# Turning the attention probabilities on VectorE in 32 by 32 blocks, value products on 32 by 64 tiles, and normalising on ScalarE

## The chip, the cores and the metric

One core of a Trainium2 chip runs the whole program. The time is the device time of one execution in microseconds. Its engines are PE (TensorE, matrix products), DVE (VectorE), ACT (ScalarE), POOL (GpSimd) and SP (SyncE, which here only starts transfers). ACT can start transfers too.

## The reference

A sequence of 512 rows of width 2048 goes through two layers of a block, and then through a recurrent mixer. The attention of a layer is what the change touches:

```python
for i in range(DEPTH):                      # DEPTH = 2
    hn = _rmsnorm(h, norm_g[i])
    u = hn @ w_in[i]
    a_val, a_glu, a_z, q, k, v, b_z = jnp.split(u, offs, axis=-1)
    ya = _conformer_conv(a_val, a_glu, conv_w[i], conv_b[i], cln_g[i], cln_b[i])
    ya = ya * jax.nn.silu(a_z)
    # 16 query heads of 64, 4 key and value heads; blocks of 128 queries see 3 blocks of keys,
    # key and query at most 128 apart
    yb = _window_attention(q, k, v, bias_band, sink[i]) * jax.nn.silu(b_z)
    h = h + jnp.concatenate([ya, yb], axis=-1) @ w_out[i]
    e = _rmsnorm(p[i] @ w_pe[i], pe_g[i])
    h = h + e * jax.nn.sigmoid(h @ w_pg[i])

# in _window_attention, for one block of queries
s = jnp.einsum('bqkgd,bskd->bkgqs', qb, kb) * scale + bias_band      # masked with NEG
m = jnp.maximum(jnp.max(s, axis=-1), sink_f)
e = jnp.exp(s - m[..., None])
denom = jnp.sum(e, axis=-1) + jnp.exp(sink_f - m)
pr = e / denom[..., None]
out = jnp.einsum('bkgqs,bskd->bqkgd', pr, vb)
```

Behind the two layers stands `h + norm(rglru(norm(h)))` (projection, short convolution, gates, a scan over the rows, projection) and one more gate.

## The kernel before

**Main products.** Everything has its channels on the 128 partitions and the 512 rows in the columns. An f32 product is made of three: weights are split into a high part `WH` and a low part `WL`, activations into `XH` and `XL`, and `three` (L1533 to L1535) or `pair_unit` (L1557 to L1563) adds high by high, low by high and high by low over 128 by 128 weight tiles and 512 columns. Weights arrive in units of 512 KB in a ring of four: SP loads `raw`, ACT writes `WH` (`prep`, L527), POOL writes `WL` (L498), PE uses the unit up and counts `w_used`. Each engine has its own list of instructions, which it works off in the order of the code; semaphores tie the lists together.

**Attention in the z stage.** While PE makes the 16 tiles of z (the gates of both halves, `silu` on them), attention goes between the main products, eight pairs of heads `t` in each layer. The stage is cut into 25 steps `n` of 10, 10 and 11 weight tiles (`Z_CUTS`). After the step with n % 3 = 0, PE makes `values(n // 3 - 1)` and then `scores(n // 3)`; after the step with n % 3 = 2 it makes `turn(n // 3)`. DVE, ACT and POOL have the same loop over n; `UNITS_AT` says which units of weights end in which step.

- `scores(t)` (PE, L1721): per block of 128 queries b and head hh, 64 by 64 tiles, 192 to 320 keys wide. The order of the blocks is `BLOCKS` (1, 2, 0, 3). Results stand in the PSUM tiles sc (b = 1), att and stat (b = 2), tr (b = 0 and 3).
- DVE adds the bias to them, finds the maximum and writes them to SBUF (L1130); ACT makes the exponentials and their sums (`exps`, L663, and the sink's, L666).
- `finish(t)` (DVE): adds the sums (L1136), takes the reciprocal (L1138) and multiplies the eight tiles of probabilities by it (L1144, L1149); each counts `probs_ready`.
- `turn(t)` (PE, L1731): 20 transposes of 128x128 against the identity, into the PSUM banks of the scores.
- `probs_out(t)` (ACT, L680 and L685): copies them to SBUF, to the turned tiles (`TX`, inside H and an own tile); `pt_ready`.
- `values(t)` (PE, L1742): 20 calls of 64 keys by 64 channels of a head. Tiles of the first 64 keys of each block add up in bank `TR[0]`, those of the last 64 in `TR[1]` (`VALUE_STEPS` gives key block and columns of each).
- `att_out` (DVE, L1153) and `far_out` (ACT, L673) copy the two sums to SBUF, and before the gate DVE adds the two (L1162). The scores of block 0 of the next pair wait for both copies (`att_ready`, `att_far`), as they use those banks.

A matmul of f32 operands (scores and values) stands twice in the records for each call. The values `v` stand turned in H (tiles `VT`, `turn_values`, L1706, copied by ACT, L653).

**Behind the z stage** the output stage adds H from memory (`h_dma` on SP, four loads of 1 MB; `add_out`, L1201) to the products of the second group of weights. The last stage, B, has its own weights; ahead of it ACT takes roots for the norm (`root`, Sqrt).

Column sums for the norms are made from squares by adding tiles on DVE; the last addition of each sum goes to the SBUF tile `acc`, from which `split_low` makes the operand SPLIT of the statistics product (`stat`, L1599).

## Time and profile before

| | before |
|---|---|
| time, median of 3 runs | 2586.24 us (2586.16 to 2586.34) |
| profiled execution | 2586.3 us |
| its span | 2584.5 us |
| PE busy | 2576.5 us, 100% |
| DVE busy | 1350.7 us, 52% |
| ACT busy | 971.2 us, 38% |
| POOL busy | 1430.0 us, 55% |
| granted clock of PE | 1.00 |

The span runs from the first to the last instruction of the profiled execution; 1.8 us lie around it. Ends of matmuls are modelled, so two matmuls overlap in the records: of main products read the starts. A row "x6" in a timeline joins six neighbours of one kind; its length is that of all six.

### The profile page before, as it was taken

The numbers are of one execution on the slowest core, as the hardware profiler recorded it, in microseconds if no ns is written. First come the engines' busy times: TensorE is split into PE (matmuls) and PEld (weight loads), VectorE is DVE, ScalarE is ACT, GpSimd is POOL, SyncE is SP. The second block draws the span as 40 slices with busy tenths as digits, with TensorE's granted clock in tenths as the row PEclk, the third lists the DMA queues.
The fourth block names the chain that finished last, engine by engine and source line by source line (L and its number), as shares of the span: only waits on it lengthen the run. The fifth ranks groups of instructions, "written<-read, shape, count | busy, mean of one in ns | idle before, by whom it ended". The sixth has DMA issues, their size and how long they took to land.

```text
span 2584.5 us, 35219 instructions
## 1 busy us (share of the span) xinstructions
PE 2576.5 (100%) x12368; PEld 2116.8 (82%) x12368; DVE 1350.7 (52%) x2086; ACT 971.2 (38%) x1516; POOL 1430.0 (55%) x1812
## 2 busy tenths in 40 slices
PE   9999999999999999999999999999999999999999
PEld 7888888788888888888887888888888888888887
DVE  7877766540063277777665400633753664522722
ACT  5222355442162242223544321733422656423521
POOL 5555545455565555555444555555666777655664
PEclk9999999999999999999999999999999999999999
DMA  7322222242234332222232422333333222322232
GB/s 249 106 98 97 94 88 94 86 154 94 95 100 136 114 123 95 94 96 98 85 97 91 151 95 97 98 130 114 106 105 123 98 98 97 140 98 97 90 98 105
DMA packets 78100, 279.34 MB, mean 108 GB/s; under 512 B 8304, under 2 KB 15216, under 8 KB 74928
## 3 DMA queue, kind: packets, MB, share of 16 engines
q1 hardware_dynamic: 77856, 277.89, 32.1%
q8 instruction: 63, 1.03, 0.2%
q14 instruction: 37, 0.30, 0.0%
q10 hardware_dynamic: 144, 0.11, 0.0%
HBM read 265.36 MB, written 15.76 MB: 109 GB/s over the span
## 4 chain that ended last, share of the span: by engine, by line
issue 36%; POOL 34%; PE 28%; POOLq 0%; DMA 0%; ACT 0%; SPq 0%; DVE 0%; DVEq 0%
POOL WL L498 34%; PE acc L1533 7%; PE acc L1534 7%; PE acc L1535 7%; PE sc L1533 1%; PE sc L1534 1%; PE sc L1535 1%; PE sc L1559 1%; PE sc L1557 1%; PE sc L1563 1%; DMA raw<-in_w 0%; PE tr L1533 0%; PE tr L1534 0%; PE tr L1535 0%; POOL WL L503 0%
## 5 line engine op out<-in xcount | busy, mean ns | idle before, releaser
L498 POOL TENSOR_TENSOR WL<-raw,WH 128x256 fp32r<-128x256 f32 x1792 | 1414.2, 822 | 1121.3 <-ACT WH L527 1121.2
L527 ACT ACTIVATE WH<-raw 128x1024 fp32r<-128x1024 f32 x450 | 472.1, 1058 | 1191.3 <-PE acc L1535 681.6
L1533 PE MATMUL acc<-XH,WH 128*128 128x512 f32 x2128 | 831.6, 391 | 0.0
L1535 PE MATMUL acc<-XH,WL 128*128 128x512 f32 x2128 | 828.2, 389 | 0.0
L1534 PE MATMUL acc<-XL,WH 128*128 128x512 f32 x2128 | 828.1, 389 | 0.0
L1533 PEld LDWEIGHTS acc<-XH,WH 128*128 128x128 f32 x2128 | 399.4, 188 | 86.5 <-issue 4.5
L1535 PEld LDWEIGHTS acc<-XH,WL 128*128 128x128 f32 x2128 | 399.4, 188 | 83.7
L1534 PEld LDWEIGHTS acc<-XL,WH 128*128 128x128 f32 x2128 | 399.5, 188 | 81.8
L1533 PE MATMUL sc<-XH,WH 128*128 128x512 f32 x640 | 249.0, 389 | 0.8 <-POOL WL L498 0.8
L1535 PE MATMUL sc<-XH,WL 128*128 128x512 f32 x640 | 249.0, 389 | 0.0
L1534 PE MATMUL sc<-XL,WH 128*128 128x512 f32 x640 | 249.0, 389 | 0.0
L943 DVE SCALAR_TENSOR_TENSOR Y<-tr,lv,Y 128x503 f32 (+13 forms) x240 | 175.6, 732 | 2.3 <-DVE T L1038 2.2
L943 DVE SCALAR_TENSOR_TENSOR T<-acc,rs 128x512 f32<-128x512 f32 (+1 forms) x78 | 53.1, 682 | 235.8 <-PE acc L1535 235.8
L943 DVE SCALAR_TENSOR_TENSOR T<-tr,lv,T 128x498 f32<-128x498 f32 (+6 forms) x224 | 163.8, 731 | 0.0
L1533 PEld LDWEIGHTS sc<-XH,WH 128*128 128x128 f32 x640 | 120.1, 188 | 26.2 <-issue 1.2
L1535 PEld LDWEIGHTS sc<-XH,WL 128*128 128x128 f32 x640 | 120.1, 188 | 25.0
L1534 PEld LDWEIGHTS sc<-XL,WH 128*128 128x128 f32 x640 | 120.1, 188 | 24.8
L1557 PE MATMUL sc<-XH,WH 128*128 128x512 f32 x320 | 98.7, 390 | 0.0
L1559 PE MATMUL sc<-XH,WL 128*128 128x512 f32 x320 | 98.5, 389 | 0.0
L1559 PE MATMUL acc<-XH,WL 128*128 128x512 f32 x320 | 98.5, 389 | 0.0
L1563 PE MATMUL sc<-XL,WH 128*128 128x512 f32 x320 | 98.5, 389 | 0.0
L1563 PE MATMUL acc<-XL,WH 128*128 128x512 f32 x320 | 98.5, 389 | 0.0
(294 smaller groups left out, 2739.9 us busy)
## 6 DMA issues: line engine op xcount, KB each, us to landing
raw<-in_w SPq DMA_DIRECT2D x450, 512.0 KB, 3.3
h_spill<-H SPq DMA_DIRECT2D x8, 1024.0 KB, 6.0
H<-h_spill SPq DMA_DIRECT2D x8, 1024.0 KB, 7.4
a<-bias_band SPq DMA_DIRECT2D x16, 384.0 KB, 3.2
H<-in_x SPq DMA_DIRECT2D x5, 1024.0 KB, 10.7
bias_band<-bias_line SPq DMA_DIRECT2D x1, 3072.0 KB, 16.1
out<-H SPq DMA_DIRECT2D x3, 1024.0 KB, 8.0
H<-in_x SPq DMA_DIRECT2D x5, 512.0 KB, 8.7
```

The lines of the kernel that those rows point to most:

```text
L498: part = pool.tensor_tensor(WL[:, c], raw[:, c], WH[:, c].bitcast(F), ALU.subtract)
L527: act.activation(WH[:, c], raw[:, c], ACT.Copy).then_inc(wh_ready, 1)
L943: return dve.scalar_tensor_tensor(out_, in0, scalar, in1, op0, op1)
L1533: pe.matmul(bank, WH[:, c], xh, start=first, stop=False)
L1534: pe.matmul(bank, WH[:, c], xl, start=False, stop=False)
L1535: return pe.matmul(bank, WL[:, c], xh, start=False, stop=last)
L1557: pe.matmul(two[b][:, :], WH[:, cols[b]], tl(XH, kt), start=first, stop=False)
L1559: pe.matmul(two[b][:, :], WL[:, cols[b]], tl(XH, kt), start=False, stop=False)
L1563: low = pe.matmul(two[b][:, :], WH[:, cols[b]], tl(XL, kt), start=False, stop=final)
```

## The change

- `turn` and `probs_out` are gone. `block_turns(t)` on DVE, in the step n % 3 = 2, turns each 32 by 32 block of the probabilities in its place (`dve.transpose`, 16 instructions a pair, 12 of 128 and 4 of 256 columns): the rows of a turned tile are then the keys of a group i of 32 within each 128, and the columns are ordered by key block, group of 32 queries and query.
- `values(t)` takes one row group of 32 partitions for each i. Row group i holds, for each group k of 32 queries, its probabilities for keys in the blocks near by, and reads `value_part(g, k)`, the values laid out for it. It makes 16 steps x 4 row groups x 2 heads = 128 calls on tiles of 32 rows by 64 columns, 32 to 96 columns wide, 992 columns in all for each tile (1088 before), into four banks `VALUE_BANKS`: att (`VB`), stat (`N`), and the two of tr.
- The layout of the values for this is made once a layer by transfers on ACT's queue (`value_copies`): one of 512 KB to `v_spill` in memory, then 12 reads, 2 MB in all, in pieces of 512 bytes; `v_out`, `vr_in`.
- The reciprocal stays on DVE (`recip_ready`), the eight multiplications go to ACT (`norms`, at the beginning of the step n % 3 = 2).
- `att_out` copies banks 0 and 1 on DVE, `far_out` banks 2 and 3 on ACT, each 128x128, straight to the tile of H. The addition L1162 is gone. The scores of block 2 wait for DVE's two, those of block 0 for ACT's two. The gated result of attention stays in H (`silu`, `xhigh`, `xlow`).
- SP: loads 2 and 3 of H in the output stage are issued behind four more weight units and a wait for `xl_ready`.
- Sums of squares stay in PSUM (`VB`) and are no longer copied to `acc`; at the start the squares are taken in another order (`X_LEAD` 11, `first_square`, `half_high`); in stage B `prep(B0, 1)` and `prep(B0, 2)` stand ahead of `root`, and `prep(B0, 3)` ahead of the second Sqrt.

The diff, without the sums and with the renamed tiles left out:

```diff
+def value_steps(i):
+
+    def seen(k):
+        near = [b for b in range(NB) if abs(4 * b + i - k) <= 4]
+        return k, near[0], near[-1] + 1
+
+    return [seen((i + s) % GROUPS_OF) for s in (12, 0, *range(1, 12), 13, 14, 15)]
...
+        def turned(hh, k, b0, b1):
+
+            o, lo, n = queries_of(k // 4)
+            c = o * BLK + (k % 4 * n + b0 - lo) * QB
+            return TX[hh][:, c:c + (b1 - b0) * QB]
+
+        def turned_to(hh, b, kb, blocks):
+
+            o, lo, n = queries_of(kb)
+            nxt = queries_of(kb + 1) if blocks == 2 else (o, lo, n)
+            step = (nxt[0] - o) * BLK + (lo - nxt[1]) * QB
+            return bass.AP(TXT[hh], o * BLK + (b - lo) * QB, [[TXW[hh], P], [step, blocks], [n * QB, 4], [1, QB]])
...
+        def value_part(g, k):
+
+            if g == 0:
+                return Y, (CT * S + k * P)
+            return (Y, 12 * S + k * P) if k < 12 else (H, VT * S + (k - 12) * P)
...
+        VALUE_BANKS = (VB, N, TR[0], TR[1])
...
                 for c in range(4):
+                    if c == 2:
+                        pair_units(u0, OUT0 + RING, OUT0 + 8)
+                        sp.wait_ge(xl_ready, ly * (3 * NT) + 2 * NT)
                     if ly:
                         sp.wait_ge(h_out[c], ly * 16)
                     h_dma(c, False, ly == 0)
-                pair_units(u0, OUT0 + RING, OUT0 + 8)
...
                 def far_out(t):
 
                     act.wait_ge(pv_done, ly * CT + (t + 1))
-                    act.activation(tl(Y, CT + t), TR[1][:, :], ACT.Copy).then_inc(att_far, 1)
-
-                def probs_out(t):
-                    base = ly * (2 * PAIRS) + 2 * NB * t
-                    for hh in range(2):
-                        for b in (0, 3):
-                            act.wait_ge(tr_done, base + 2 * hh + 2)
-                            act.activation(turned_of(b, hh), sbank(b, hh).rearrange("p (k q) -> p k q", q=BLK),
-                                           ACT.Copy).then_inc(pt_ready, 1)
-                    for b in (1, 2):
+                    for i in (2, 3):
+                        act.activation(att_part(t, i), VALUE_BANKS[i][:, 0:BLK].rearrange("p (b q) -> p b q", q=QB),
+                                       ACT.Copy).then_inc(att_far, 1)
+
+                def norms(t):
+                    act.wait_ge(recip_ready, ly * CT + (t + 1))
+                    st = sm[:, 24 * (t % 2):24 * (t % 2) + 24]
+                    for c, b in enumerate(BLOCKS):
                         for hh in range(2):
-                            act.wait_ge(tr_done, base + (2 * b + hh + 3))
-                            act.activation(turned_of(b, hh), sbank(b, hh).rearrange("p (k q) -> p k q", q=BLK),
-                                           ACT.Copy).then_inc(pt_ready, 1)
+                            k = 8 + 4 * hh + c
+                            act.activation(pbuf(b, hh), pbuf(b, hh), ACT.Copy, scale=st[:, k:k + 1]).then_inc(probs_ready, 1)
+
+                def value_copies():
+
+                    act.wait_ge(v_out, ly * 16 + 16)
+                    for g in range(2):
+                        for i in range(4):
+                            for kb0, kb1 in ((0, 4),) if g == 0 else ((0, 3), (3, 4)):
+                                buf, c = value_part(g, 4 * kb0)
+                                act.dma_start(buf[i * QB:(i + 1) * QB, c:c + (kb1 - kb0) * S].rearrange("p (k c) -> p k c", c=P),
+                                              bass.AP(v_dram, kb0 * BLK * 2 * P + g * P,
+                                                      [[2 * P, QB], [QB * 2 * P, 4 * (kb1 - kb0)], [1, P]])).then_inc(vr_in[g], 16)
 
                 values_out(0)
                 values_out(1)
+                act.wait_ge(v_ready, ly * 2 + 2)
+                act.dma_start(bass.AP(v_dram, 0, [[2 * P, P], [BLK * 2 * P, NB], [1, 2 * P]]),
+                              H[:, VT * S:(VT + 2) * S].rearrange("p (k c) -> p k c", k=NB)).then_inc(v_out, 16)
                 for n, ended in enumerate(UNITS_AT):
...
                             exps(n // 3)
-                    elif n % 3 == 2:
-                        probs_out(n // 3)
+                    if n == 0:
+                        value_copies()
...
+            prep(B0, 1)
+            prep(B0, 2)
             root(tl(T, 5), DEPTH * 4 + 1, 1.0 / D)
-            prep(B0, 1)
+            prep(B0, 3)
             act.wait_ge(fvar_ready, 1)
             act.activation(rs[:, :], tl(T, 4), ACT.Sqrt, bias=eps[:, 0:1], scale=1.0 / D).then_inc(root_ready, 1)
-            prep(B0, 2)
...
@@ -1135,34 +1170,35 @@
                     dve.wait_ge(exp_done, ly * CT + (t + 1))
                     did(dve.tensor_tensor(st[:, 8:16], st[:, 8:16], st[:, 16:24], ALU.add))
                     settle()
-                    did(dve.reciprocal(st[:, 8:16], st[:, 8:16]))
-                    settle()
-                    for hh in range(2):
-                        for c in (2, 3):
-                            k = 8 + 4 * hh + c
-                            pb = pbuf(BLOCKS[c], hh)
-                            dve.tensor_scalar(pb, pb, st[:, k:k + 1], None, ALU.mult).then_inc(probs_ready, 1)
-                    for c in (0, 1):
+                    dve.reciprocal(st[:, 8:16], st[:, 8:16]).then_inc(recip_ready, 1)
+
+                def block_turns(t):
+                    base = ly * (2 * PAIRS) + 2 * NB * t
+                    if t:
+                        dve.wait_ge(pv_done, ly * CT + t)
+                    for c, b in enumerate(BLOCKS):
                         for hh in range(2):
-                            k = 8 + 4 * hh + c
-                            pb = pbuf(BLOCKS[c], hh)
-                            dve.tensor_scalar(pb, pb, st[:, k:k + 1], None, ALU.mult).then_inc(probs_ready, 1)
+                            dve.wait_ge(probs_ready, base + 2 * c + hh + 1)
+                            for kb, blocks in {0: ((0, 1), (1, 1)), 1: ((0, 1), (1, 2)), 2: ((1, 2), (3, 1)), 3: ((2, 1), (3, 1))}[b]:
+                                m = (kb - keys_of(b)[0]) * BLK
+                                last = dve.transpose(turned_to(hh, b, kb, blocks), pbuf(b, hh)[:, m:m + blocks * BLK])
+                            last.then_inc(pt_ready, 1)
 
                 def att_out(t):
                     dve.wait_ge(pv_done, ly * CT + (t + 1))
-                    dve.tensor_copy(tl(H, QT + t), TR[0][:, :]).then_inc(att_ready, 1)
+                    for i in (0, 1):
+                        dve.tensor_copy(att_part(t, i), VALUE_BANKS[i][:, 0:BLK].rearrange("p (b q) -> p b q", q=QB)).then_inc(att_ready, 1)
 
                 def silu(j):
 
                     dve.wait_ge(z_th, ly * NT + (j + 1))
...
@@ -1710,9 +1745,10 @@
                     for b in BLOCKS:
                         if b == 0 and t == 0:
                             pe.wait_ge(v_ready, ly * 2 + 2)
+                        elif b == 2:
+                            pe.wait_ge(att_ready, 2 * (ly * CT + t))
                         elif b == 0:
-                            pe.wait_ge(att_ready, ly * CT + t)
-                            pe.wait_ge(att_far, ly * CT + t)
+                            pe.wait_ge(att_far, 2 * (ly * CT + t))
                         for hh in range(2):
                             r = slice(hh * DH, (hh + 1) * DH)
                             for c in range(2):
@@ -1722,25 +1758,18 @@
                                                  tl(H, KT + t // GQ)[r, k0:k1], start=True, stop=True)
                             last.then_inc(scores_done, 1)
 
...
-                    for n, both in enumerate(zip(*VALUE_STEPS)):
-                        for r, (kb, q0, q1) in enumerate(both):
-                            rows = slice(r * HB, (r + 1) * HB)
-                            o = queries_of(kb)[1] * BLK
+                    if t % GQ == 0:
+                        pe.wait_ge(vr_in[t // GQ], 64 * (1 + t // GQ) * (ly + 1))
+                    for n, each in enumerate(zip(*(value_steps(i) for i in range(4)))):
+                        for i, (k, b0, b1) in enumerate(each):
+                            rows = slice(i * QB, (i + 1) * QB)
+                            buf, c = value_part(t // GQ, k)
                             for hh in range(2):
-                                v0 = VT * S + kb * 2 * P + (2 * (t // GQ) + hh) * DH
-                                last = pe.matmul(TR[r][hh * DH:(hh + 1) * DH, q0:q1], H[rows, v0:v0 + DH],
-                                                 turned(kb, hh)[rows, q0 - o:q1 - o], start=n == 0, stop=n == len(VALUE_STEPS[0]) - 1)
+                                last = pe.matmul(VALUE_BANKS[i][hh * DH:(hh + 1) * DH, b0 * QB:b1 * QB],
+                                                 buf[rows, c + hh * DH:c + (hh + 1) * DH], turned(hh, k, b0, b1)[rows, :],
+                                                 start=n == 0, stop=n == GROUPS_OF - 1)
                     last.then_inc(pv_done, 1)
```

On PE the turn stood between two main products of tile z, here in pair 0 of the first layer; `a`, `acc`, `H` hold the probabilities, `ident` is the identity, out is the PSUM tile.

```order
L1535 MATMUL acc<-XH,WL 128x512
L1731 MATMUL tr<-ident,a 128x128 [waits probs_ready]
L1731 MATMUL tr<-ident,a 128x128
L1731 MATMUL tr<-ident,a 128x128 [waits probs_ready]
L1731 MATMUL tr<-ident,a 128x128
L1731 MATMUL tr<-ident,a 128x128 [waits probs_ready]
L1731 MATMUL tr<-ident,a 128x128
L1731 MATMUL tr<-ident,acc 128x128 [waits probs_ready]
L1731 MATMUL tr<-ident,acc 128x128
L1731 MATMUL sc<-ident,H 128x128 [waits probs_ready]
L1731 MATMUL sc<-ident,H 128x128 x2
```

These 20 transposes and their loads are gone from PE; the main products above and below are neighbours now.

The values of pair 0 on PE, before:

```order
L1535 MATMUL acc<-XH,WL 128x512
L1742 MATMUL tr<-H 64x320 [waits pt_ready]
L1742 MATMUL tr<-TX_56,H 64x320
L1742 MATMUL tr<-H 64x320
L1742 MATMUL tr<-TX_56,H 64x320
L1742 MATMUL tr<-H 64x192
L1742 MATMUL tr<-TX_56,H 64x192
```

and now (`H` and `TX_56` are the turned probabilities of the two heads, `Y` the values as laid out):

```order
L1570 MATMUL acc<-XH,WL 128x512
L1770 MATMUL att<-H,Y 64x64 [waits vr_in0,pt_ready]
L1770 MATMUL att<-TX_56,Y 64x64
L1770 MATMUL stat<-H,Y 64x64
L1770 MATMUL stat<-TX_56,Y 64x64
L1770 MATMUL tr<-H,Y 64x64
L1770 MATMUL tr<-TX_56,Y 64x64
L1770 MATMUL tr<-H,Y 64x64
L1770 MATMUL tr<-TX_56,Y 64x64
```

The names of the out tiles go round four banks instead of two, and there are 128 such calls in a row instead of 20.

On DVE, around the end of the softmax of one of the pairs of the first layer (`T` and `Y` belong to the gates, `sm` holds sums and reciprocals), before:

```order
L943 SCALAR_TENSOR_TENSOR T<-acc,rs 128x512 [waits w_used]
L1136 TENSOR_TENSOR sm<-sm 128x8 [waits exp_done]
L1138 RECIPROCAL sm<-sm 128x8 [waits dve_chain]
L1144 TENSOR_SCALAR a<-a,sm 128x256 [waits dve_chain]
L1144 TENSOR_SCALAR a<-a,sm 128x256 x2
L1144 TENSOR_SCALAR acc<-acc,sm 128x256
L1149 TENSOR_SCALAR H<-H,sm 128x384 x2
L1149 TENSOR_SCALAR a<-a,sm 128x384 x2
L943 SCALAR_TENSOR_TENSOR T<-T 128x512 [waits z_th]
```

and now:

```order
L1171 TENSOR_TENSOR sm<-sm 128x8 [waits exp_done]
L1173 RECIPROCAL sm<-sm 128x8 [waits dve_chain]
L980 SCALAR_TENSOR_TENSOR T<-T 128x512 [waits z_th]
L1201 TENSOR_TENSOR Y<-Y,T 128x512 [waits dve_chain]
L980 SCALAR_TENSOR_TENSOR Y<-Y,lv,T 128x512 [waits dve_chain]
L1147 TENSOR_SCALAR Y<-Y,lv 128x512 [waits dve_chain]
L1184 STREAM_TRANSPOSE H<-H 128x4x32 [waits probs_ready]
L1184 STREAM_TRANSPOSE H<-H 128x2x4x32
L1184 STREAM_TRANSPOSE TX_56<-H 128x4x32 [waits probs_ready]
```

The multiplications behind the reciprocal are gone; the turns stand behind the silu and the layer norm step, ahead of the swish and of the read of the next finished tile.

On ACT, in the first pair of a layer, now:

```order
L690 ACTIVATE sm<-sm,der 128x4 x2
L716 DMA Y<-v_spill 32x16x128 [waits v_out]
L716 DMA Y<-v_spill 32x16x128 x3
L716 DMA Y<-v_spill 32x12x128
L716 DMA H<-v_spill 32x4x128
L716 DMA Y<-v_spill 32x12x128
L716 DMA H<-v_spill 32x4x128
L716 DMA Y<-v_spill 32x12x128
L716 DMA H<-v_spill 32x4x128
L716 DMA Y<-v_spill 32x12x128
L716 DMA H<-v_spill 32x4x128
L551 ACTIVATE WH<-raw 128x1024 [waits w_used,raw_in1]
```

Twelve transfers stand between the exponentials and the split of a weight unit, and the scalings ahead of the next split, where before copies of the turned tiles stood.

## Rows read from the trace of the kernel before

**Rows 1.** The page: busy time and instructions; granted clock in 40 slices

```profile
PE 2576.5 (100%) x12368; PEld 2116.8 (82%) x12368; DVE 1350.7 (52%) x2086; ACT 971.2 (38%) x1516; POOL 1430.0 (55%) x1812
...
PEclk9999999999999999999999999999999999999999
```

**Rows 2.** Waits of PE: waiting, waited for, us in all, times, longest

```profile
PE tr L1605 <- DVE Y L960: 1.5, 1, 1.5
PE sc L1533 <- POOL WL L498: 0.8, 1, 0.8
```

**Rows 3.** PE's timeline, turn of pair 4: start, length, line, out<-in, count

```profile
447.26 0.39 PE L1535 MATMUL acc<-XH,WL 128*128 128x512 f32 x1
...
447.94 0.39 PE L1535 MATMUL acc<-XH,WL 128*128 128x512 f32 x1
448.18 0.81 PE L1731 MATMUL tr<-ident,a 128*128 128x128 f32 x6
...
452.90 0.39 PE L1535 MATMUL acc<-XH,WL 128*128 128x512 f32 x1
```

**Rows 4.** PE's timeline, values of pair 3

```profile
430.28 0.39 PE L1535 MATMUL acc<-XH,WL 128*128 128x512 f32 x1
430.60 0.48 PE L1742 MATMUL tr<-H 64*64 64x320 f32 x1
...
431.52 0.22 PE L1742 MATMUL tr<-H 64*64 64x64 f32 x1
...
431.54 0.22 PE L1742 MATMUL tr<-TX,H 64*64 64x64 f32 x1
431.57 0.22 PE L1742 MATMUL tr<-H 64*64 64x64 f32 x1
...
432.50 0.72 PE L1721 MATMUL sc<-H 64*64 64x320 f32 x8
```

**Rows 5.** Timeline of all engines, scores of pair 4, 433.30 to 433.60

```profile
432.74 0.69 DVE L1153 COPY H<-tr 128x512 f32<-128x512 f32 x1 [4.06 <-PE tr L1742]
433.04 0.44 PE L1721 MATMUL att<-H 64*64 64x320 f32 x2
...
433.49 0.24 PEld L1721 LDWEIGHTS tr<-H 64*64 64x64 f32 x8 [0.30 <-DVE H L1153]
```

**Rows 6.** DVE's timeline, pair 3, 405 to 430.5

```profile
408.20 0.48 DVE L1130 CUSTOM_DVE_ANT_0 a<-tr,a,lv 128x256 f32<-128x256 f32 x1
...
408.60 0.48 DVE L1130 CUSTOM_DVE_ANT_0 a<-tr,a,lv 128x256 f32<-128x256 f32 x1
...
412.52 0.20 DVE L1138 RECIPROCAL sm<-sm 128x8 f32<-128x8 f32 x1
412.76 2.20 DVE L1144 TENSOR_SCALAR a<-a,sm 128x256 f32<-128x256 f32 x3
...
420.44 0.69 DVE L943 SCALAR_TENSOR_TENSOR T<-T 128x512 f32<-128x512 f32 x1 [0.70 <-ACT T L697]
```

**Rows 7.** ACT's timeline, pair 3, exponentials of L663, sinks of L666

```profile
406.70 0.62 ACT L663 ACTIVATE H<-H,sm 128x384 f32<-128x384 f32 x1 [0.74 <-DVE sm L1130]
...
411.08 0.47 ACT L666 ACTIVATE sm<-sm,der 128x4 f32<-128x4 f32 x2
```

**Rows 8.** DMA issues, 320 to 345 and 550 to 572: KB, us to landing

```profile
a<-bias_band SPq DMA_DIRECT2D x1, 384.0 KB, 3.3
...
H<-in_x SPq DMA_DIRECT2D x4, 1024.0 KB, 9.6
```

**Rows 9.** DVE's timeline, output stage, 565 to 590

```profile
585.87 1.28 DVE L1201 TENSOR_TENSOR H<-H,acc 128x512 f32 x2 [19.20 <-PE acc L1563]
```

**Rows 10.** Waits of PE's weight loads

```profile
PEld stat L1599 <- DVE SPLIT L952: 1.1, 2, 0.5
```

**Rows 11.** Queue q8 and the engines in the window 322.9 to 541.9

```profile
q8 instruction: 12, 0.20, 0.4%
...
322.90:541.90 219.00, 219.00 (x1481) 176.22 (x1480) 137.73 (x296) 114.60 (x278) 101.48 (x124) 1.00 0.27 88
```

90 lines of the change are left out of this document (36 added, 54 removed).

## The prediction

> **What bounds the kernel now.** I read the page's first two sections, then the waits of PE, then PE's timeline around one pair of heads, and only then the other engines. The reader is to see first that PE is the whole span: 2576.5 of 2584.5 us busy, at the full granted clock (PEclk 9 in every slice) [rows 1]. All that PE waits for comes to some 3 us; the largest entries are 1.5 us at the start and 0.8 us for a POOL result near 1849 [rows 2]. So a microsecond taken out of PE's own list is a microsecond off the time, as long as nobody becomes late; work taken off DVE, ACT or POOL is worth nothing by itself. The profiled execution took 2586.3 us, span 2584.5 and 1.8 around it; the median of the runs is 2586.24, so I sum against 2586.3 and read the result as the median.
>
> **Turning the probabilities on PE goes.** Of one turn (pair 4 of layer 0) the timeline shows the last main product starting at 447.94 and twenty transposes from 448.18 (five rows, of which the first stands) [rows 3]. Main products start 0.227 us apart when undisturbed (three steps from 447.26 to 447.94). The twelfth main start after the turn is at 452.90: 4.96 us for twelve steps, which alone take 12 x 0.227 = 2.72. The turn costs 2.24 us. Sixteen of them: **-35.8 us**. It is all on PE's path, so nothing covers it and nothing else has to fall for it to be gained.
>
> **Value products on 32 by 64 tiles.** Before, 40 matmul records of 64x64 tiles run from 430.60 to the first score at 432.50, 1.90 us [rows 4]; they stream 1088 columns through each of four tiles. Four starts of 64 columns, 431.52, are followed by the next four at 431.57: 0.055 us, two cycles of 2.4 GHz a column, and each call is issued twice. So 1088 x 4 / 2.4 GHz = 1.81 us: the array sets this time, with 5% on top. Now eight tiles work side by side (4 row groups, 2 heads), 992 columns in each, 128 calls in 16 steps. As the steps keep their order over the tiles, the widest tile sets a step: two steps of 96 columns and fourteen of 64 or less. A 64-column step takes 2 x 0.055 us [rows 4], with some overhead 0.114. So 14 x 0.114 + 2 x 0.165 = 1.93 us, with the few per cent of before's overhead some 1.95: **+0.05 each, +0.8 in all**. The bound below is 992 x 4 / 2.4 = 1.65 us, -4 in all.
>
> Values and scores now use different tile shapes, so the engine changes shape once more per pair. From a main product to the first value takes 0.32 us against 0.227 [rows 4]: +0.10 each, **+1.6**; between 0 and 3 in all.
>
> **Instructions.** The same columns now come in 512 instructions (128 calls, each issued twice, each with a weight load) where 80 did, less the turn's 40. What one costs when the array isn't the limit no row shows directly. The nearest: after the copy L1153 ended at 433.43, eight weight loads start within 433.49 to 433.60 and the four matmuls between them too [rows 5]; at least 15 instructions had passed 0.17 us after the release, so **at most 11 ns each**. In [rows 4] the four starts of a 64-column step lie between 431.52 and 431.54, some 7 ns apart. The new code needs 1.95 us / 512 = 3.8 ns per instruction, 7.6 ns per start. From below, nothing excludes that it is hidden altogether (cost 0); from above stand the 11 ns. I take "hidden", since the four starts in a step have that pitch with their loads between; the other end makes two rivals.
>
> **Waits of the scores for the copies.** Results of values lie in four banks; the scores of block 2 wait for two DVE copies of 128x128, and those of block 0, later, for ACT's. Before, one copy of 512 columns ran from 432.74, 0.24 us after the scores had begun, to 433.43 and let block 0 start at 433.49 with no loss [rows 5]. Block 2 comes 0.54 us after the scores' begin. Two copies of 128 columns take, each half to all of the 0.40 us between two reads of 256 columns (408.20, 408.60) [rows 6], 0.4 to 0.8 us. I take 0.5: ready at 0.75 to 0.8, **+0.25 us for 14 pairs, +3.5** (a layer's first pair has no such wait). Range 0 to +9. What is queued behind the waiting score is all of PE's list.
>
> **DVE and ACT around it.** DVE loses the eight multiplications (the first three take 2.20 us from 412.76 [rows 6]; all eight some 5) and gets 16 block transposes, 12 of 128 and 4 of 256 columns. By that same pitch of 0.40 for 256 columns, and 0.27 for 128: 4.8 us; at half that rate some 8.2 to 9.6. ACT loses eight copies of the turned tiles and gets eight scalings; the eight exponentials of the same shapes took 406.70 to 411.08, 4.4 us with their reads [rows 7]; scalings some 3.6. For the tightest pair (3) the reciprocal is at 412.52, so ACT scales from 413.1 to 416.7, then does its weight split and tanh; DVE's silu (420.44 before [rows 6], held by ACT) and the three operations behind it end at about 421.5, and block_turns runs from there to 426.3. PE wants the result at 428.4 (430.60 less the turn). **Margin about 2 us, cost 0**; at half the rate a stall of 1.3 to 2.7 us for this pair, and less for the others, whose DVE has less beside it: 3 to 9 us in all. Behind block_turns on DVE stand a swish and the read of a finished tile; before, that read waited for PE, so there is room. The add L1162 goes, off the path: 0.
>
> **The values' copies.** One write of 512 KB and 12 reads with 2 MB in 512-byte pieces from ACT's queue, once a layer. 384 KB landed in 3.3 us [rows 8]. The first four reads, all that the first four pairs need, have 1 MB: by that rate 9 us at most if nothing runs beside, issued at about 332 they land near 341, wanted at 346 (the first values). Twelve issues hold ACT for some 5 us behind the exponentials, before its scalings at 337: cost 0, bound 3 per layer. The loads of H for output tiles 2 and 3 stand on SP's queue behind four more weight units and a wait for xl_ready: issue about 571, 9.6 us at most to land [rows 8], 581; PE wants the sums at 585.87 [rows 9]. Margin 5 us, cost 0. Weight units move ahead of them, which helps.
>
> **Small edits.** Near 1849 PE waits 0.8 us for WL [rows 2] because a ScalarE root stands ahead of the weight split; the order is turned round: **-1.0** (with the slow restart behind the wait), and 0 at worst. Column sums kept in PSUM shorten the way to the statistics products, whose weight loads wait for DVE's SPLIT 1.1 us in two places [rows 10]; half of that is **-0.5**, between -1.1 and 0. The other order of the squares at the start: 0, between -0.7 and +0.7, as the chain there has about 2 us of room.
>
> Sum: -35.8 + 0.8 + 1.6 + 3.5 - 1.0 - 0.5 = -31.4; 2586.3 - 31.4 = **2555**. By the bounds, 2547 to 2565.
>
> **Rivals.**
> (C, by a page.) The Trainium skill, "TensorE: Matmul & The Clock Gate", section "Wait — 56ns, not 53.3ns?", says that matmul starts never come closer than about 25 ns, however few the columns; a rule that speaks against this change: by it values would take an estimated 256 x 25 = 6.4 us and the kernel some 2626. The trace doesn't agree for different tiles: 7 ns between starts, 14 on average [rows 4].
>
> (C) *Dispatch is the bound*, at PE's values. The forecast leaves 31.4 / 16 = 1.96 us a pair; it is used up when values take 3.9 us, that is from 7.6 ns per instruction on (3.9 / 512). At the upper bound of 11 ns a pair takes 5.6 us, 3.7 more than forecast, x 16 = +59: **2614**, slower; from 7.9 ns up to that, 2590 to 2614. For it: no row shows a long run of matmuls so dense, the densest have sixteen. Against: the pitch of 7 ns with loads between, and 11 ns is only what the latency behind the release lets one see. 21%.
>
> (B) *Supply of instructions, middling.* In 219 us of the attention stage 12 packets of instructions arrive for 1481 matmuls and as many loads, 247 a packet; 0.4% of 16 engines' 219 us over 12 is 1.2 us each [rows 11]. Two packets' worth now pass in 1.95 us. If one is fetched only while the one before it runs, each falls 0.2 us behind at best and, if the fetch begins late, 0.6: +0.5 to +1.2 a pair, 2563 to 2574; 6 ns of dispatch give 3.1 us, +18, 2573. **2562 to 2580**, 20%.
> The Trainium skill, "Runtime: NRT & Kernel Launch", section "Instruction fetch mechanics", has blocks of 16 KiB (256 instructions) fetched while the current one runs, and calls that hidden because dispatch is slower; by it B gives nothing and the forecast stands, but its reason doesn't hold at 3.8 ns an instruction. The trace agrees on the size, 247 a packet.
>
> (D) *It doesn't do what it says*: a row group of 32 can't work beside another of its half, two of four at a time. Values take 3.8 us, +1.9 x 16 = +30: **2585**, within 0.2%. Nothing in the trace shows tiles of 32 rows in number. 6%.
>
> (E) *The new chain is late* (reciprocal, scaling on ACT, block_turns on DVE at the slow rate above, or ACT's twelve issues ahead of it): **2558 to 2570**, 2564. 5%.
>
> **How the numbers follow.** (A) the forecast, 48%; B 20%, E 5%, D 6%, C 21%. The time is that of A, **2555**. A measurement here can tell about 0.2%, 5 us, from no change. Faster: A + B + E = 0.73; same: D = 0.06; slower: C = 0.21. A alone spans 2547 to 2565. The range reaches over B, D and E into C and leaves out A's low end (3%) and the larger part of C (15%): **2549 to 2600**.
>
> **What would show it.** In PE's timeline: no transposes between main products; values from first record to first score in 1.9 to 2.0 us with eight starts per 0.055 us. Starts at an even pitch of 14 ns or more, whatever the width, would be C; gaps of a microsecond at irregular places, with a q8 packet ending there, B; steps twice as long, D; "idle before <- DVE" at the first value record, E. A wait of 0.2 to 0.3 us on DVE's copy ahead of the scores of block 2 shows my +3.5. The forecast is wrong if values take more than 3 us, whatever the cause.

## The result and the profile after

The changed kernel takes 2626.1 us (median of 4 runs, 2622.7 to 2630.1) against 2586.3 before: the ratio is 1.0154, interval 1.0138 to 1.0171. It is slower by 40 us where 31 us less were forecast, and the time lies outside the range. The profiled execution is the shortest of the four, 2622.7 us.

The page of the changed kernel (busy time; granted clock in 40 slices; the queue of the instructions) beside [rows 1]:

```profile
PE 2580.0 (98%) x15504; PEld 2120.9 (81%) x15504; DVE 1316.2 (50%) x2214; ACT 983.9 (38%) x1532; POOL 1416.2 (54%) x1812
...
PEclk9999999999999999999899999999999999999999
...
q8 instruction: 87, 1.43, 0.2%
```

PE is still busy nearly all the time, but it now makes 15504 matmuls instead of 12368, its span is 2620.9 us, it idles 41 us, one slice of the clock reads 8, and 87 packets of instructions came where 63 did. What it waits for (columns as in [rows 2]):

```profile
PE tr L1770 <- issue: 15.7, 8, 3.6
PE stat L1770 <- issue: 8.6, 4, 2.7
PE att L1770 <- issue: 8.0, 4, 3.1
PE att L1770 <- DVE TX L1184: 2.5, 2, 2.0
PE tr L1640 <- DVE Y L997: 1.5, 1, 1.5
```

32 us are "issue": no semaphore that the profile shows holds the value products (L1770), and still they don't start. It happens 16 times, once a pair. The timeline of PE through the values of pair 1 of layer 0 (start, length, line; the counterpart of [rows 4]):

```profile
375.69 0.27 PE L1770 MATMUL att<-H,Y 32*64 32x64 f32 x1
...
376.06 0.26 PE L1770 MATMUL stat<-H,Y 32*64 32x64 f32 x1
```

```profile
377.32 0.24 PE L1770 MATMUL att<-TX,Y 32*64 32x96 f32 x1
...
379.12 0.27 PE L1770 MATMUL att<-TX,Y 32*64 32x64 f32 x1 [1.41 <-issue]
...
380.25 0.77 PE L1757 MATMUL sc<-H 64*64 64x320 f32 x8
```

The first record is at 375.69, and 163 of the 256 start by 377.48; the next one, at 379.12, was held by "issue"; the first score is at 380.25. The values took 4.56 us instead of 1.90. The same stretches with their counts of matmuls (columns: stretch, its length, busy time and count of PE, granted clock, share of the transfers, GB/s; a matmul that is still running from the stretch before is counted again):

```profile
375.69:377.48 1.79, 1.79 (x164) 1.00 0.41 117
377.48:379.12 1.64, 0.24 (x19) 1.00 0.59 200
379.12:380.25 1.13, 1.13 (x94) 1.00 0.07 18
```

Without the stall of 1.64 us (377.48 to 379.12) the 256 starts take 2.92 us, 11.4 ns each. That is the second loss. The transfers, from 375.69 to 376.70 and, the second row, from 376.70 to 377.75:

```profile
DMA packets 0, 0.00 MB, mean 0 GB/s; under 512 B 0, under 2 KB 0, under 8 KB 0
```

```profile
q8 instruction: 1, 0.02, 5.7%
```

Until 376.70 nothing arrives at all. Then one packet of instructions (16 KB) comes, beside a transfer of weights, and PE goes on at 379.12, 1.4 us after its end. In the records the stalls stand behind matmul 162 of this pair (counted from 0), 164 of the next, 166, and so on to 174, and in layer 1 behind 197 to 211. The count moves by two matmuls, four instructions, a pair (by one to three in the records, of which some are missing). So does a border that comes every 256 instructions: a pair has 764 of them, four less than three times 256 (93 main, 256 value and 32 score matmuls with their loads are 762, and the trace has two or three semaphore instructions beside them). So each stall is put at the second border inside the values; the first one, 128 matmuls earlier, here at 376.06, has passed without a halt. From the first border to the end of the stall it is 376.06 to 379.12, **3.06 us**; the other pairs show 3.1 to 5.2. The transfer of the packet begins 0.7 to 3.0 us after the first border, takes 0.9 to 1.5, and PE goes on 1.2 to 1.6 us after its end. The sixteen stalls, from start to start of the matmuls around them, sum to 35.9 us; the 32 us of the waits leave out the modelled length of the matmul before each.

The third loss is the clock. The values of pair 2, which have a stall of 2.3 us in them, and two stretches behind them (columns as above):

```profile
403.66:409.10 5.44, 3.35 (x258) 0.94 0.37 102
409.10:411.00 1.90, 1.90 (x19) 0.50 0.00 0
...
412.44:414.00 1.56, 1.56 (x11) 1.00 0.08 16
```

At 409.10, where the scores begin, the granted clock is 0.50, which is 1.2 GHz, and the scores take 3.34 us (409.10 to 412.44) instead of 2.11 in pair 1. Before, the clock was at this level once, at the very end of the span; now it is so in ten of the sixteen pairs as well, all of them with stalls above 1.8 us (behind two stalls of that size, and the four shorter ones, it stayed up). In nine it falls behind the stall; in the first pair of layer 1 it falls at 1268.62, ahead of the stall, 0.7 us after PE has ended a wait of 2 us for the block turns.

Where the 36.4 us of the span came from: the two z stages (first score to last value) took 236.1 and 238.2 instead of 219.0 each, +36.3; the start is 2.4 shorter and the rest 2.4 longer, nearly all of it behind the z stage of layer 0, where the clock is at its lower level up to 562.1. Inside the z stages: turns -35.8, stalls +35.9, slower values +18.6 (49.1 us without stalls against 30.5; 16 times 2.92 are 46.7, and two pairs with part of their values at the lower clock have most of the rest), and +17.6 in the scores and the main products behind them: some 2.3 for the wait on DVE's copies, 2.5 for the late first pairs (the DVE row above), and the 13 or so that remain, not measured by themselves, are put down to the low clock.

### The profile page after: what moved, and what is told of

Read it like the earlier page. It is cut to its first block, busy times and chain, and to the rows that moved or that the text cites. A ratio compares the mean times of both kernels' runs of the same rounds, so it can differ in the third digit from the quotient of the medians.

```text
span 2620.9 us, 41666 instructions
## 1 busy us (share of the span) xinstructions
PE 2580.0 (98%) x15504; PEld 2120.9 (81%) x15504; DVE 1316.2 (50%) x2214; ACT 983.9 (38%) x1532; POOL 1416.2 (54%) x1812
## 4 chain that ended last, share of the span: by engine, by line
PE 97%; issue 1%; DVE 1%; ACT 1%; ACTq 1%; DVEq 0%
PE acc L1568 18%; PE acc L1569 18%; PE acc L1570 18%; PE sc L1568 6%; PE sc L1569 6%; PE sc L1570 6%; PE sc L1592 3%; PE sc L1594 3%; PE sc L1598 3%; PE acc L1592 3%; PE acc L1594 3%; PE acc L1598 3%; PE tr L1770 1%; PE tr L1568 1%; PE tr L1569 1%
## 5 line engine op out<-in xcount | busy, mean ns | idle before, releaser
L1569 PE MATMUL acc<-XL,WH 128*128 128x512 f32 x2128 | 828.5, 389 | 0.0
L1239 DVE TENSOR_TENSOR H<-H,sc 128x512 f32 x16 | 10.3, 684 | 179.3 <-PE sc L1598 117.4
```

The costliest lines, as they stand in the source:

```text
L1239: dve.tensor_tensor(tl(H, t), tl(H, t), OUT_BANKS[j][:, :], ALU.add).then_inc(tile_out, 1)
L1569: pe.matmul(bank, WH[:, c], xl, start=False, stop=False)
```

## The experiments

Where no interval is given, an experiment was run once. In the diffs "..." marks lines left out.

**Old calls, new chain.** The changed kernel, with 20 value calls of 64 by 64 tiles as before, on the same tiles (its result is not the reference's):

```diff
-                    for n, each in enumerate(zip(*(value_steps(i) for i in range(4)))):
-                        for i, (k, b0, b1) in enumerate(each):
+                    for n, both in enumerate(zip(*VALUE_STEPS)):
+                        for r, (kb, q0, q1) in enumerate(both):
...
```

> The changed kernel with all of its chain (scaling on ACT, block turns on DVE, value copies, waits of the scores, small edits), but the value products made in the old 20 calls of 64 by 64 tiles on the same tiles, so that their result is not what the reference wants. Theory: nothing but the number of instructions makes the loss, so this one is as fast as the forecast said: 2586.3 - 35.8 (turns) + 2.3 (scores' wait, 0.16 us x 14) + 2.5 (the first pair's late chain) - 1.5 (small edits) = 2554 (2550 to 2558). Rival: the chain on DVE and ACT, or the transfers, hold PE up: above 2565.

Measured: 2556.2 us (before, beside it, 2585.9). The forecast's own terms give what they were to give: turns gone, DVE, ACT and the transfers no burden. PE's waits:

```profile
PE att L1774 <- DVE TX L1186: 3.7, 2, 2.8
PE tr L1642 <- DVE Y L999: 1.5, 1, 1.5
```

Only the first pair of each layer waits for the block turns, 3.7 us. What makes the changed kernel slower than before sits in the 128 calls.

**Only the number of calls.** The kernel before, with value calls cut to 32 columns:

```diff
+QC = 32
...
-                    for n, both in enumerate(zip(*VALUE_STEPS)):
+                    cut = [[(kb, q, q + QC) for kb, q0, q1 in steps for q in range(q0, q1, QC)] for steps in VALUE_STEPS]
+                    for n, both in enumerate(zip(*cut)):
...
```

> The kernel before, with turns on PE, 64 by 64 tiles and all its waits, but the value products cut into calls of 32 columns: 136 calls instead of 20, 544 instructions instead of 80, the same 1088 columns. Theory (instructions): one stall of 1.5 to 3.8 us a pair as in the changed kernel though nothing else of it is there, and 272 starts 11 ns apart, 3.1 us instead of 1.9: +1.2 + 2.2 + 0.5 (clock) a pair, 2586 + 16 x 3.9 = 2648 (2635 to 2660). Rival (the 32-row tiles, or the new transfers and chain, make the loss): values stay at 1.9 to 2.0 us and the kernel at 2586 to 2590. If only supply counts and not the feeding, +2.2 to 3.2 a pair with starts at the array's pace: 2621 to 2640.

Measured: 2654.2 us, +68. PE's waits, and in its timeline the record behind one of the stalls:

```profile
PE tr L1744 <- issue: 18.9, 15, 2.1
```

```profile
386.02 0.24 PE L1744 MATMUL tr<-TX,H 64*64 64x32 f32 x1 [1.50 <-issue]
```

The kernel of before with nothing else changed has such stalls too, 1.0 to 2.3 us in fifteen of the sixteen pairs, 22 us in all, and needs 4.1 us for the rest of its values. They stand where a border every 256 instructions would put them: a pair has 837 instructions here, 69 more than three times 256, and the stalls of the first four pairs stand behind matmul 268, 234, 199 and 165, that is 34 to 35 matmuls earlier each time (in the first pair of layer 1 the border has moved into the scores, with a stall of 1.3 us there). From the first border to the end of the stall it is 2.9 to 4.2 us here. So tiles of 32 rows, the chain and the transfers are not needed for the loss. The rest is larger than the 3.1 expected: four starts take 58 ns, 14.6 each, 7.3 ns an instruction, more than the 5.2 that PE takes further below (e2, e6). So feeding isn't what paces them; that it is the four tiles, each with a new weight load before each product, is what is left, and not tested by itself.

**Halves.** The changed kernel, the values in steps 0 to 7 and 8 to 15, three weight tiles of main products between:

```diff
+                        if n % 3 == 1 and n > 1 and (kt - Z_CUTS[n] + 1) % 3 == 0:
+                            part = (kt - Z_CUTS[n] + 1) // 3
+                            if part <= 1:
+                                values(n // 3 - 1, part)
+                                if part == 1:
+                                    scores(n // 3)
...
-                    if n % 3 == 0:
-                        if n:
-                            values(n // 3 - 1)
-                        if n // 3 < CT:
-                            scores(n // 3)
...
+                    elif n % 3 == 0:
+                        values(n // 3 - 1, 0)
```

> The changed kernel, with the 128 value calls in two halves and three weight tiles of main products (2.04 us) between them. My theory now: PE gets its instructions in packets of 256; the next packet is asked for only when the first instruction of the last one that is there is reached, and it is there 3.1 to 3.7 us later. The 512 instructions of the values take 2.9 us, so the second border inside them is reached too early and PE stands for 1.6 to 3.8 us once a pair (36 us in all), after which the granted clock is low for a while. With 2.04 us more between the two borders the stall goes nearly always: at most 0.3 us left a pair where a fetch takes 3.1 us, up to 0.9 where it takes longer. Sum: 2626 - 34 (stalls) - 14 (clock at its lower level) + 5 (one more change of the tile shape a pair) = 2580 to 2584, faster than the changed kernel by 1.7% and within 0.3% of before. Rival: the stall belongs to the value products (a queue of PE that fills with small matmuls, or the weight transfers that run at that time): it stays, at the same count of matmuls, and the time is 2620 to 2632.

Measured: 2584.8 us, 0.9996 of before (0.9986 to 1.0005), 41 us less than the changed kernel with the same instructions. PE's waits, and pair 1 in windows (first half, pause, second half):

```profile
PE att L1775 <- DVE TX L1184: 4.1, 2, 2.1
PE tr L1640 <- DVE Y L997: 1.5, 1, 1.5
PE tr L1775 <- issue: 1.1, 1, 1.1
PE tr L1757 <- issue: 1.0, 3, 0.5
```

```profile
375.09:376.67 1.58, 1.58 (x130) 1.00 0.42 65
376.67:378.93 2.26, 2.26 (x15) 1.00 0.49 190
378.93:380.43 1.50, 1.50 (x129) 1.00 0.06 16
```

The stalls are gone but for 2.5 us, and the clock is low in two stretches instead of ten, each right behind the wait of some 2 us for the block turns in the first pair of a layer. The pace within a half is about as before, 11.7 ns a start (1.50 us for 128, with the step to the scores). The rival, that the stall belongs to the value products, falls.

**One tile between.** The same with one weight tile (0.68 us) instead of three.

```diff
-                        if n % 3 == 1 and n > 1 and (kt - Z_CUTS[n] + 1) % 3 == 0:
+                        if n % 3 == 1 and n > 1 and (kt - Z_CUTS[n] + 1) % 1 == 0:
...
```

> The values in two halves with one weight tile between them (0.68 us) instead of three. It asks whether the stall is a fixed time from border to border. In the changed kernel the second border is reached some 1.45 us after the first and PE goes on 3.1 us after it at best (3.7 to 5.2 in the disturbed pairs). With the pause and its changes of shape (0.68 + 0.4) the second border comes at about 2.5 us: the stall of each pair should shrink by about 1.1 us, to 0.5 to 1.2 in the undisturbed pairs, some 13 us of stalls in all instead of 36; the kernel near 2600 (2592 to 2606). If the stall had to do with how many small products stand in a row (it ended with three tiles between), it would be gone here too: 2585 or less. If only full separation helps: 2625.

Measured: 2601.5 us. The stalls shrink but stay:

```profile
PE tr L1775 <- issue: 7.0, 7, 2.1
PE stat L1775 <- issue: 6.9, 6, 2.1
PE att L1775 <- DVE TX L1184: 3.9, 2, 2.3
PE att L1775 <- issue: 2.6, 3, 1.6
```

They sum to 20.0 us instead of 35.9, 0.6 to 1.3 in twelve pairs and 1.9 to 2.4 in four; 16.5 us of "issue" are named in the waits. So it is the time from border to border that counts, and not how long a row of small products is. The four pairs whose fetches take longer have most of the 7 us by which the sum of the stalls is above what was expected.

**What paces the starts.** Three kernels that leave work out, so that their results are not the reference's: all calls 32 columns wide (e2); weight tiles 32 channels wide (e6); one head only (e5).

```diff
+                            b1 = b0 + 1
```

```diff
-                                last = pe.matmul(VALUE_BANKS[i][hh * DH:(hh + 1) * DH, b0 * QB:b1 * QB],
-                                                 buf[rows, c + hh * DH:c + (hh + 1) * DH], turned(hh, k, b0, b1)[rows, :],
+                                last = pe.matmul(VALUE_BANKS[i][hh * DH:hh * DH + 32, b0 * QB:b1 * QB],
+                                                 buf[rows, c + hh * DH:c + hh * DH + 32], turned(hh, k, b0, b1)[rows, :],
```

```diff
-                            for hh in range(2):
+                            for hh in range(1):
```

> The changed kernel, but each of the 128 value calls is only 32 columns wide (instead of 32 to 96); the values' result is incomplete. It asks what limits the values outside the one stall: 2.93 us for 256 matmul records where 1.95 were forecast. If the feeding of instructions limits (11.4 ns a matmul with its load), the time without the stall stays 2.9 us, the stall stays where it is, and the kernel takes 2620 to 2630. If the array limits (32-row tiles stream slower than 64-row ones), the time falls with the columns, to about half, 1.5 us, and the stall grows by what is saved, since the packet comes no earlier: 2610 to 2630 for the kernel. So the time doesn't tell, the pitch of the starts in PE's timeline does.

> The changed kernel, all 128 calls with their columns, but each weight tile only 32 channels wide instead of 64 (half of the result is missing). Same number of instructions. If feeding paces the values, they keep their 2.9 us without the stall and the kernel stays at 2620 to 2632. If the weight loads pace them (they take time by their width), they fall to the 1.8 to 2.0 us of the array, while the stall grows by as much, as its end is set by the arrival of the packet: again 2615 to 2632 in time, but starts 7 ns apart.

> The changed kernel with the value products of one of the two heads left out: 64 calls, 128 matmuls, 256 instructions a pair, on four tiles of 32 rows instead of eight; columns of each tile as before. It asks what paces the starts at 11.4 ns. If the feeding of instructions does (5.7 ns each), a pair takes half, 1.5 us, or 1.8 to 1.9 us by the array, which needs 2 x 0.055 us for a step of 64 columns; if each row group takes its weight loads and products one after the other (0.18 us a step of two heads), also half. If every tile has a floor of its own between two products (0.09 us), the values stay at 2.9 us. With one border of a packet inside instead of two the long stalls go; kernel at 1.5 to 1.9 us a pair: near 2556 (2550 to 2562), at 2.9 us near 2572.

Measured: 2636.2, 2624.1 and 2556.9 us. Pair 1 in windows (in e2 and e6 up to the stall, in e5 the whole pair), beside 1.79 us for the same 164 matmuls of the changed kernel:

```profile
377.41:379.01 1.60, 1.60 (x164) 1.00 0.54 74
```

```profile
377.42:379.07 1.65, 1.65 (x164) 1.00 0.37 129
```

```profile
371.25:373.35 2.10, 2.10 (x130) 1.00 0.46 133
```

With half the columns (e2) the 164 take 1.60, with half the width of the loads (e6) 1.65: both change 8 to 11% where halves were at stake. Without stalls both need 2.67 us for 256 starts, 10.4 ns each or **5.2 ns an instruction**. With half the instructions (e5) the values take 2.1 us and no long stall is there; there an instruction comes every 8.2 ns, so it is not the feeding that paces, and each tile starts 64 columns every 0.06 us, as the array did before. So with eight tiles the number of instructions sets the pace, and neither width does. Some 0.25 us come on top (2.92 against 2.67), which go when either width is halved; what they are is open. Whether the 5.2 ns lie in the sequencer or in the queue ahead of the array, these runs can't tell. e2 was above the 2630 expected: its stalls sum to 41.7 us against 35.9, and its mean granted clock is 0.985.

**The late first pair.** In the changed kernel ACT's timeline shows the twelve reads of the values being issued ahead of a weight split (start, length; ACTq is the issuing):

```profile
325.54 0.88 ACTq L716 DMA_DIRECT2D Y<-v_spill  x2
...
329.72 1.75 ACTq L716 DMA_DIRECT2D Y<-v_spill  x1
...
334.38 0.71 ACTq L716 DMA_DIRECT2D H<-v_spill  x1
335.20 1.06 ACT L551 ACTIVATE WH<-raw 128x1024 fp32r<-128x1024 f32 x1 [6.74 <-issue]
```

From 325.54 to 335.09, 0.8 us for each with ACT's other work between them, the split behind them waits 6.74 us, and the scaling and block turns behind that. The experiment is e1 with eight of the reads in two later lots:

```diff
-                        value_copies()
+                        value_copies(0, range(4))
+                    if n in (4, 7):
+                        value_copies(1, range(2) if n == 4 else range(2, 4))
```

> The kernel with the values in two halves (e1), and eight of the twelve reads of the laid-out values, those that only pairs 4 to 7 need, issued on ACT later in two lots of four (steps 4 and 7) instead of all twelve ahead of the first scaling. PE waited 4.1 us in e1 for the first block turns of both layers, since ACT came 3.5 us late out of the issues. Theory: that wait goes, 2584.8 - 4 = 2580.5 (2578 to 2583). Rival: the lots only move the delay to later pairs, or the wait is the chain's own: 2583 to 2587.

Measured: 2577.8 us (2576.0 to 2578.8), **0.9968 of before** (0.9955 to 0.9980). PE's waits:

```profile
PE tr L1642 <- DVE Y L999: 1.5, 1, 1.5
PE tr L1759 <- issue: 0.8, 3, 0.3
```

The wait for DVE is gone. The gain over e1 is 7 us where 4 were expected; the rest is two stretches at the low clock and a stall of 1.3 us that e1's profile has and this one has not. This version is faster than both kernels.

**Only the borders moved.** f1, with two of the four warm-up products replaced by 48 tiny ones:

```diff
-            for _ in range(WARM):
+            for _ in range(WARM - 2):
                 pe.matmul(TR[1][:, :], tl(Y, 0)[:, 0:P], tl(Y, 0), start=True, stop=True)
+            for _ in range(48):
+                pe.matmul(TR[1][0:32, 0:16], tl(Y, 0)[:, 0:32], tl(Y, 0)[:, 0:16], start=True, stop=True)
```

> f1 with nothing changed but where the borders of the instruction packets fall: two of the four warm-up products at the start are replaced by 48 tiny ones, 184 instructions more, which moves each border 92 matmuls earlier, modulo 128. In e1 the pairs of layer 0 (border 33 to 47 matmuls into each half, a third border in the scores right behind) spent 0.1 to 0.9 us more after the second half than those of layer 1 (border at 70 to 84). Theory: with layer 0 at 69 to 83 and layer 1 at 106 to 120 both behave like layer 1: 3 us less than f1, 2577 (2574 to 2579). Rival (the position doesn't matter): the same as f1 within 1 us, or up to 1.5 slower from the start.

Measured: 2576.9 us (2576.0 to 2580.7), no difference from f1 that can be told. The stages say more, with a reserve: the profiled execution is the slowest of the five, 2580.7 us. In it layer 0's z stage falls from 217.6 to 213.8 us, as expected, but layer 1's grows from 214.0 to 216.9, where stalls of 0.1 to 1.2 us stand behind matmul 96 to 102 of the second half in the first four pairs, and the start is 4.7 us longer. The stages are shorter or longer with the position of the borders, so it seems to matter; as three of the five executions are at 2576.0 to 2576.9, some of the losses in layer 1 and at the start must be this execution's own, and how much is open.

**Four tiles between**, instead of three, in f1:

```diff
-                        if n % 3 == 1 and n > 1 and (kt - Z_CUTS[n] + 1) % 3 == 0:
+                        if n % 3 == 1 and n > 1 and (kt - Z_CUTS[n] + 1) % 4 == 0:
...
```

> f1 (halves, late reads) with four weight tiles between the halves instead of three. In f1 the pairs of layer 0 spend some 3.8 us more than those of layer 1 (the z stage took 217.6 against 214.0), as their third packet border lies in the scores right behind the second half. Theory: 0.68 us more between the halves doesn't change the way from the second border to the third, but gives the slow fetches (up to 4.4 us) inside the halves room; so little changes: 2577.8 - 0.5 = 2577 (2575 to 2579). Rival: the margin of DVE's chain (2.6 us at pair 3 of layer 1, less 2.7 now) is used up and PE waits for block turns in two pairs: 2579 to 2582.

Measured: 2578.0 us (2576.5 to 2579.3), as f1; the z stages are 217.5 and 213.8. Neither more room inside nor the shorter margin of DVE makes a difference that can be told.

**The small edits alone**, on the kernel before (order of the squares, sums in PSUM, stage B's order), a line or two of each:

```diff
-        X_LEAD, BESIDE = 5, 3
+        X_LEAD = 11
...
-            dve.tensor_tensor(acc[:, :], VB[:, :], rs[:, :], ALU.add).then_inc(hsum_ready, 1)
+            dve.tensor_tensor(VB[:, :], VB[:, :], rs[:, :], ALU.add).then_inc(hsum_ready, 1)
...
+            prep(B0, 1)
+            prep(B0, 2)
             root(tl(T, 5), DEPTH * 4 + 1, 1.0 / D)
```

> The kernel before with only the small edits: the other order of the squares at the start, the column sums kept in PSUM, and the weight splits of stage B ahead of the roots. Forecast for them was -1.5 us (-1.0 in stage B, -0.5 at the statistics, 0 at the start). In the traces of the changed kernel and its variants the first scores begin at 320.5 to 321.4 instead of 322.9, and the rest behind layer 1 is 1.1 shorter (1134.0 against 1135.1). Theory: the small edits give all of that, 1.5 to 2.4 at the start and 1.1 behind: 2586.1 - 3.1 = 2583 (2582.3 to 2583.7). Rival (the start's gain comes from the moved value transfers or from chance of the profiled runs): 2584.6.

Measured: 2583.3 us, 0.9989 of before (0.9980 to 0.9999). PE's waits are down to one row:

```profile
PE tr L1602 <- DVE Y L962: 1.5, 1, 1.5
```

They are worth 2.9 us, of which the forecast had 1.5.

## Why the prediction was wrong

The steps that failed are *Instructions*, put at 0, and the supply of rival B, put at 8 to 19 us: they cost 16 and 36 us, and the low clock behind the stalls came on top. Of the signs named, that of B is there (gaps with a q8 packet ahead of their end, though at regular places), and the values take more than 3 us.

- *Turning on PE goes*: -35.8 held. e4 bears it out: 2585.9 - 35.8 + 4.2 (scores' waits, 0.3 x 14) + 3.7 (first pairs) - 2.9 (small edits, e8) = 2555.1, and it measured 2556.2.
- *Instructions*: here it failed. The 11 ns were taken as a bound, the 7 ns of [rows 4] as proof that 7.6 ns a start could be had. Four starts in a row don't show what a long run gets. In pair 1 the first 32 starts lie between 375.69 and 375.95, and 32 again between 379.12 and 379.39 behind the stall, some 8.5 ns apart; over all 256 they come every 11.4 ns. It looks as if a stock of instructions is used up first. The term was 0 and should have been +1.0 us a pair (2.92 against 1.95, x 16 = +16). As values and scores follow each other without a pause, nothing hid it.
- *Supply*, rival B, had the right mechanism and too small a price. It counted the packet alone, 1.2 us [rows 11]. From the first border the transfer begins 0.7 us later at best, takes 0.9 to 1.5, and PE goes on some 1.4 us after its end: 3.06 us or more, for 256 instructions that the values use up in 1.45. That is a stall of at least 1.6 us a pair, +26, and +36 as measured, where the text had +8 to +19. B and C were kept apart (B's 6 ns of dispatch, values at 3.1 us, +18, stood beside its fetch and were not added to it), but both came: +36 and +16 turn -31 into +21 without the clock. With some 15 for the clock, 2 for values at its lower level and 2.5 for the first pairs, less 4 in the small terms below, the sum is +36, the difference of the two spans.
- The clock stood in no term: stalls of 2 us and more were not foreseen, and some 13 us in the z stages and 2 behind them are put down to it. In e1, with the stalls gone, the time fell by 41 us where the stalls had 33 of it.
- The rule of the Trainium skill ("TensorE: Matmul & The Clock Gate", section "Wait — 56ns, not 53.3ns?") that starts stay some 25 ns apart gave an estimate of 2626, which is what was measured, but by luck and not by its mechanism: starts are 11.4 ns apart here, and 10.4 in e2. Of the section "Instruction fetch mechanics" of the Trainium skill ("Runtime: NRT & Kernel Launch"), the trace agrees on 256 instructions (the stalls stand at such borders) and not on their being hidden.
- *Value tiles*: the array's part can't be read from the changed kernel, as feeding covers it; e5, with the same steps on one head's tiles, has 2.1 us where the forecast had 1.95. Row groups of 32 do work side by side (in the first steps eight tiles start within 0.06 us), so D is out. The change of shape cost nothing: 0.32 us from the last main product to the first value as in [rows 4], and 0.15 from the last value to the first score against 0.14. Forecast +1.6.
- *Waits of the scores*: 0.16 us a pair without stalls (f1), 0.3 in e4, for 0.25 forecast.
- *DVE and ACT*: no cost but in the first pairs, and none was forecast; the turns are cheaper than the 4.8 us assumed:

```profile
L1184 DVE STREAM_TRANSPOSE H<-a 128x128 f32<-128x128 f32 x80 | 19.0, 267 | 0.0
...
L1184 DVE STREAM_TRANSPOSE H<-a 128x256 f32<-128x256 f32 x16 | 6.4, 399 | 0.0
```

  Busy 0.27 and 0.40 us, but the starts follow at 0.19 and 0.33: 3.7 us a pair, done 2.6 to 7.8 us ahead of the values except in the first pair of a layer.
- *The values' copies*: the twelve issues were put at 5 us "behind the exponentials" with no cost. They took 9.6, and PE waited 2.5 us for what stood behind them (4.1 in e1), within the bound of 3 a layer; f1, where eight of them come later, has no such wait. The transfers themselves and the moved loads of H held nobody.
- *Small edits*: -2.9 instead of -1.5; the start was to give 0 and gave 1.4, the whole difference.
- *Range*: the lower bounds of all terms sum to 2544 and not to 2547, and the upper ones to 2564 only without the 6 us for ACT's issues; neither would have reached 2626.

## What to carry to other kernels

Count the instructions of a dense stretch as well as its columns: here a run of 512 went in at 5.2 ns each at best, and every 256 of them need some 3 us or more of time since the last 256, which small products don't fill. Where a rewrite makes many small calls out of few large ones, spread them between large products (2 us between two halves gave 41 us back), and look for "issue" as the releaser in the waits of PE. A stall has a second price, as the clock may be at its lower level behind it (scores of 3.34 us instead of 2.11).

## What the runs showed of the hardware

- Fetching instructions: a packet of 16 KB, 256 instructions (stalls move by 2 matmuls a pair with 764 instructions, by 34 to 35 with 837); from border to resumption 3.06 us at best in the changed kernel, 2.9 in e3. In the slowest pair, 5.2 us, the transfer began 3.0 us after the border, and weight transfers held the DMA engines for 0.63 of that time. The first border inside the values passes and the second doesn't, so one packet was ahead.
- Feeding PE: 10.4 ns for a matmul with its load over 256 of them, with half the columns (e2) as with half the width of the loads (e6); four starts in different tiles may stand 7 ns apart within that.
- Four tiles of 64 by 64 with new weights for each product started every 58 ns with 32 columns (e3), about what 64 columns took before (0.055 us), so halving the columns gained nothing.
- The granted clock fell to 0.50 in ten of sixteen pairs, in nine behind PE's stall, in one behind a wait of 2 us for DVE; the scores took 3.34 us behind a stall for 2.11 at 1.00.
- Issuing one of the value reads on ACT's queue costs ACT 0.45 to 1.75 us.
